# A hybrid convolution decoder step on one core: a reciprocal in three pieces and another order of low parts, weight sums and swishes

## What is computed

```python
proj = jnp.einsum('btd,de->bte', z, w_in)
a_val, a_glu, a_gate, b_h, b_c, b_b, b_gate, m_a, m_b = jnp.split(proj, SPLIT_IDX, axis=-1)
u_a = a_val * jax.nn.sigmoid(a_glu)
c_a, new_buf_a = causal_dwconv(buf_a, u_a, conv_a_w)          # width 31
c_a = layernorm(c_a + conv_a_b, ln_a_g, ln_a_b)
y_a = jax.nn.silu(c_a) * jax.nn.silu(a_gate)
u_b = b_c * b_h
c_b, new_buf_b = causal_dwconv(buf_b, u_b, conv_b_w)          # width 3
y_b = b_b * c_b * jax.nn.silu(b_gate)
merged = (jax.nn.sigmoid(m_a) * jnp.einsum('btc,cd->btd', y_a, w_pa)
          + jax.nn.sigmoid(m_b) * jnp.einsum('btc,cd->btd', y_b, w_pb))
h = h + jnp.einsum('btd,de->bte', merged, w_out)
```

## Time and profile before

| | |
|---|---|
| median of 3 runs | 1069.04 us (1068.72 to 1070.01) |
| the profiled execution | 1069.02 us |
| its span in the profile | 1067.2 us |
| instructions in the span | 19847 |
| granted clock of PE over the span, share of full speed | 0.992 |
| chain that ended last, share of the span | PE 85%, DVE 5%, DMA 3%, ACT 3%, issue 2% |
| DMA | 181.03 MB, mean 170 GB/s |

### The profile page before, as it was taken

One profiled execution on the slowest core, in us unless ns is written; L12 is line 12 of the kernel. 1 busy time (PEld: TensorE's weight loads), 2 busy tenths in 40 slices (PEclk: granted clock), 3 DMA queues, 4 the chain that ended last, 5 costly groups with the idle time before them and its releaser, 6 DMA issues.

```text
span 1067.2 us, 19847 instructions
## 1 busy us (share of the span) xinstructions
PE 1025.9 (96%) x7948; PEld 998.0 (94%) x7948; DVE 829.4 (78%) x904; ACT 471.8 (44%) x725; POOL 519.0 (49%) x369
## 2 busy tenths in 40 slices
PE   5899999999999999999999999799998988999997
PEld 5899999999999999999999999799998988998885
DVE  6779989899998989899996674875595489765523
ACT  7654343434434343433444555556463354242311
POOL 3166566565655656566563553445564456420000
PEclk9999999999999999999999999899998999999999
DMA  8677666657656665665656464584946646455321
GB/s 266 173 163 182 153 170 156 170 128 192 154 149 175 157 168 130 186 157 147 173 149 204 140 211 138 180 272 156 316 149 216 211 120 208 154 195 177 119 81 41
DMA packets 183535, 181.03 MB, mean 170 GB/s; under 512 B 9135, under 2 KB 145455, under 8 KB 182404
## 3 DMA queue, kind: packets, MB, share of 16 engines
q1 hardware_dynamic: 168468, 152.50, 44.5%
q0 software_dynamic: 14976, 27.27, 14.2%
HBM read 118.46 MB, written 35.00 MB: 144 GB/s over the span
## 4 chain that ended last, share of the span: by engine, by line
PE 85%; DVE 5%; DMA 3%; ACT 3%; issue 2%; POOL 1%; SPq 1%; ACTq 0%; DVEq 0%
PE pp L2020 74%; PE pp L2180 8%; DMA sgb<-m_spill 2%; DVE big L1506 1%; DVE xop L1469 1%; PE pp L2037 1%; POOL wop L918 1%; PE spare L2196 1%; DVE big L1948 1%; ACT wop L1017 1%; DVE ring L1664 1%; DVE x_stage L1458 1%; DMA x_stage<-in_x_prompt_dram 1%; ACT wop L985 0%; ACT xop L1001 0%
## 5 line engine op out<-in xcount | busy, mean ns | idle before, releaser
L2020 PE MATMUL pp<-xop,wop 128*128 128x262 f32 (+1 forms) x7224 | 892.1, 285 | 22.1 <-issue 7.5
L2020 PEld LDWEIGHTS pp<-xop,wop 128*128 128x128 f32 x7224 | 885.3, 190 | 26.8 <-issue 15.8
L918 POOL TENSOR_TENSOR wop<-ring,wop 128x512 fp32r<-128x512 f32 (+1 forms) x256 | 442.4, 1733 | 389.3 <-ACT wop L985 384.8
L985 ACT ACTIVATE wop<-ring 128x512 fp32r<-128x512 f32 (+1 forms) x262 | 181.6, 698 | 233.0 <-PE pp L2020 232.9
L1575 DVE SCALAR_TENSOR_TENSOR big<-big,cst 128x513 f32<-128x513 f32 x112 | 107.8, 963 | 0.7
L2180 PE MATMUL pp<-xop,wop 128*128 128x512 f32 x384 | 89.2, 394 | 0.0
L2180 PEld LDWEIGHTS pp<-xop,wop 128*128 128x128 f32 x384 | 72.0, 188 | 16.8
L1586 DVE SCALAR_TENSOR_TENSOR spare<-big,tap_sum,spare 128x512 f32<-128x512 f32 x112 | 83.7, 748 | 0.3
L1575 DVE SCALAR_TENSOR_TENSOR spare<-big,cst,spare 128x512 f32<-128x512 f32 x112 | 83.6, 746 | 0.0
L1677 DVE TENSOR_TENSOR big<-big,pp 128x524 f32<-128x524 f32 (+1 forms) x43 | 29.8, 693 | 45.9 <-PE pp L2020 45.1
L1664 DVE TENSOR_TENSOR ring<-ring 128x512 f32<-128x512 f32 x68 | 64.3, 985 | 0.0
(11 more groups left out here) (127 smaller groups left out, 713.5 us busy)
## 6 DMA issues: line engine op xcount, KB each, us to landing
ring<-in_w_in_dram SPq DMA_DIRECT2D x222, 256.0 KB, 3.3
ring<-ring POOLq DMA_DIRECT2D x104, 256.0 KB, 4.4
big<-c_spill SPq DMA_DIRECT2D x16, 516.0 KB, 5.1
big<-yb_spill SPq DMA_DIRECT2D x5, 1032.0 KB, 9.5
big<-ya_spill SPq DMA_DIRECT2D x5, 1032.0 KB, 8.0
m_spill<-big SPq DMA_DIRECT2D x16, 262.0 KB, 4.4
yb_spill<-big SPq DMA_DIRECT2D x8, 516.0 KB, 5.4
c_spill<-big SPq DMA_DIRECT2D x8, 516.0 KB, 4.5
```

The costliest lines, as they stand in the source:

```text
L918: G.tensor_tensor(wop[:, s0:s1, 1, :], raw, f(wop[:, s0:s1, 0, :]), ALU.subtract).then_inc(wlo, 1)
L985: A.activation(wop[:, s0:s1, 0, :], raw, ACT.Copy).then_inc(whi, 1)
L2020: last = T.matmul(out, wop[:, s, wp, P * k:P * (k + 1)], xop[s][:, xp, k, n * ch:n * (ch + 1)], start=(s in FRESH and k == 0 and m == 0), ...
```

## The change

It changes the order of instructions on ACT and DVE in units 29, 30, 35, 36, 39 and 40, and splits one instruction in three.

- The reciprocal at the end of unit 29 is made in three pieces of 344 columns, each of which waits for its own third of the square roots. The multiply of the first normalize_c waits for all three.
- In unit 30 norm_swish(0) and norm_swish(1) move on ACT: the first from ahead of the wait for slot 1 to behind act_first (ahead of the fourth snapshot), the second from ahead of the third snapshot to behind w_hi(31, 3).
- In units 35 and 39 x_high(p, 0) moves on ACT ahead of the first snapshot. On DVE x_low(p, 0) moves ahead of c11, and x_sum(p, 2) from ahead of c22 to behind it.
- In units 36 and 40 weight_sum 0 for the next unit moves behind x_low(p, 4), weight sums 1 to 3 from behind c11 to behind c22 (and the multiply that follows it), x_low(p, 5) ahead of the multiply that follows c11, and x_low(p, 6) ahead of the multiply and the sums that follow c22.

```diff
--- before.py
+++ after.py
@@ -1303,6 +1303,10 @@
                 more = v < NU
                 if kind == "short":
                     conv_begin(i)
+                if u == NZ - 1:
+                    x_high(1, 0)
+                if u == NPB - 1:
+                    x_high(2, 0)
                 first_product(u)
                 if u == 1:
                     x_high(0, 4)
@@ -1319,20 +1323,14 @@
                     square_row(4)
                 if n == 4:
                     square_row(7)
-                if n == 5:
-                    norm_swish(0)
                 if n == 6:
                     norm_swish(3)
                 if n == 7:
                     norm_swish(5)
                 if n == 8:
                     norm_swish(7)
-                if u == NZ - 1:
-                    x_high(1, 0)
                 if u == NZ:
                     x_high(1, 5)
-                if u == NPB - 1:
-                    x_high(2, 0)
                 if u == NPB:
                     x_high(2, 5)
 
@@ -1354,8 +1352,6 @@
                     mean_row(1)
                 if n == 3:
                     square_row(5)
-                if n == 5:
-                    norm_swish(1)
                 if u == NZ - 1:
                     x_high(1, 1)
                 if u == NPB - 1:
@@ -1371,6 +1367,8 @@
                     stage_sigmoids(i, 1)
                 if n == 1:
                     mean_row(2)
+                if n == 5:
+                    norm_swish(0)
                 if n == 2:
                     square_row(2)
                 if n == 3:
@@ -1392,6 +1390,7 @@
                 if more:
                     w_hi(v, 3)
                 if n == 5:
+                    norm_swish(1)
                     norm_swish(2)
                 if n == 6:
                     norm_swish(4)
@@ -1831,7 +1830,7 @@
                     w_low(5)
                 if u > 1:
                     after_c21(u - 1)
-                if VSUM <= u + 1 < NU:
+                if VSUM <= u + 1 < NU and u not in (NZ, NPB):
                     weight_sum(u + 1, 0)
                 if kind == "gate":
                     conv_b(i)
@@ -1848,23 +1847,27 @@
                     normalize_c(1)
                 if u == NZ - 1:
                     x_sum(1, 1)
+                    x_low(1, 0)
                 if u == NPB - 1:
                     x_sum(2, 1)
+                    x_low(2, 0)
                 if u == NZ:
                     x_low(1, 4)
+                    weight_sum(u + 1, 0)
                 if u == NPB:
                     x_low(2, 4)
+                    weight_sum(u + 1, 0)
 
 
                 c11(u)
                 if u == 1:
                     x_low(0, 5)
-                after_c11(u)
                 if u == NZ:
                     x_low(1, 5)
                 if u == NPB:
                     x_low(2, 5)
-                if VSUM <= u + 1 < NU:
+                after_c11(u)
+                if VSUM <= u + 1 < NU and u not in (NZ, NPB):
                     for step in (1, 2, 3):
                         weight_sum(u + 1, step)
                 if kind == "gate":
@@ -1892,13 +1895,9 @@
                 if n == 8:
                     gate_c(6)
                 if u == NZ - 1:
-                    x_low(1, 0)
                     x_low(1, 1)
-                    x_sum(1, 2)
                 if u == NPB - 1:
-                    x_low(2, 0)
                     x_low(2, 1)
-                    x_sum(2, 2)
 
                 if u == LAST:
                     wo_low(0)
@@ -1911,7 +1910,14 @@
                 c22(u)
                 if u == LAST:
                     wo_low(3)
+                if u == NZ:
+                    x_low(1, 6)
+                if u == NPB:
+                    x_low(2, 6)
                 after_c22(u)
+                if u in (NZ, NPB):
+                    for step in (1, 2, 3):
+                        weight_sum(u + 1, step)
                 if kind == "short":
                     sample_a(i)
                 if spread:
@@ -1919,13 +1925,11 @@
                 if n == 8:
                     gate_c(7)
                 if u == NZ - 1:
+                    x_sum(1, 2)
                     x_sum(1, 3)
                 if u == NPB - 1:
+                    x_sum(2, 2)
                     x_sum(2, 3)
-                if u == NZ:
-                    x_low(1, 6)
-                if u == NPB:
-                    x_low(2, 6)
 
 
                 c12(u)
@@ -1944,9 +1948,11 @@
                     add_square(5)
                     center(7)
                 if n == 4:
-                    dve.wait_ge(std_ready, 3)
-                    V.reciprocal(rstd, rstd).then_inc(rstd_ready, 1)
-                    dve.wait_ge(rstd_ready, 1)
+                    n3 = TOK // 3
+                    for ch in range(3):
+                        dve.wait_ge(std_ready, ch + 1)
+                        V.reciprocal(rstd[:, n3 * ch:n3 * (ch + 1)], rstd[:, n3 * ch:n3 * (ch + 1)]).then_inc(rstd_ready, 1)
+                    dve.wait_ge(rstd_ready, 3)
                     normalize_c(0)
                 if n == 5:
                     gate_c(1)
```

## The result

The changed kernel takes 1078.16 us (median of 4 runs, 1076.94 to 1079.07), the kernel before beside it 1069.53 (1068.72 to 1071.81): 1.0064 times as long, 95% interval 1.0048 to 1.0080, some 6.9 us; the two medians by themselves are 8.6 apart. Predicted were 1075.1, in 1066.0 to 1079.5, and slower as the likeliest case. The profiled execution took 1079.07, 10.05 more than that of before, with a span of 1077.2 and a mean granted clock of 0.985.

What follows compares the result with a forecast made beforehand. PE was busy 96% of the span, so only its idle time could be won, stage by stage. Terms -0.6 + 2.9 + 3.8 = +6.1 on 1069.04 gave 1075.1 us, range 1066.0 to 1079.5.

Steps and rivals of the forecast that it cites:

- Units 29 and 30, -0.6: Product 4 of unit 30 on time, product 6 idle 4.3 behind c22, clock halved; -0.6 us in all.
- POOL's turns: Unit 30: DVE and POOL alternate at the port; POOL's weight parts add 1.2 to the subtract, 2.3 to the multiply.
- A split: Unit 30: DVE and POOL share port bandwidth instead of turns; unit 30 ends near 678.5, the whole at 1070.4 us.
- Rival (a): Unit 30: normalize_c(2)'s subtract reaches the port before POOL, -5.1 instead of -0.6; 1070.6 us, chance 0.18.
- its bound of -5.1: Units 29 and 30: with the subtract ahead of POOL, idle before product 6 is 1.9, the clock holds, -5.1 us.
- Units 35 to 38, +2.9: Late weight sums hold SP's sigmoid loads; PE idles 5.2 before product 2 of unit 37, clock falls; +2.9 us.
- Rival (b): Staged-sigmoid loads of units 36 to 38 land in 2.6: +2.9 becomes -0.8, +3.8 becomes -0.5; 1067.1 us, chance 0.14.
- Units 39 to 41, +3.8: x_high(2,0) delays 39/2, late sums delay load_old(0) and merges: +2.8 with clock held, +1.0 for the clock; +3.8 us.
- the clock at 39/2: Product 2 of unit 39: after 3.8 of idle a clock fall costs 2.0; half taken, +1.0 us.
- The bounds between which I put that chance: Unit 39: idle of 3.8 lies between 2.1, which held the clock, and 4.33, which did not.
- the load: Unit 40: load_old(0) goes at 902.0 instead of 897.31, lands 907.4, delaying the merges and 41/3; +2.8 with clock held.
- Rival (c): Nothing queues behind the late sums and all places gain: -5.1, -3.5 and -2.4; 1058 us, chance 0.10.

Runs made afterwards that it cites:

- p1_c22_first: Kernel before with only the part of units 29 and 30, plus normalize_c(2) moved behind c22 on DVE in unit 30: 1065.48 us, ratio 0.9943.
- a_whi3_late: Changed kernel with ACT's w_hi(31, 3) moved behind norm_swish(2), making POOL's weight parts late: 1075.46 us, ratio 1.0026 to the kernel before.
- p3_only: Kernel before with only the change's part of units 36 and 40 (low parts ahead of weight sums): 1077.95 us, ratio 1.0070.
- a_sgb_first: Changed kernel with SP's store and staged-sigmoid loads of unit 36 ahead of the rb21 and rb22 loads: 1077.23 us, ratio 1.0062 to the kernel before.
- best4: Changed kernel with best3's SP and quadrant order, c22 ahead of normalize_c(2), load_old(0) ahead of rb21, x_high(2,0) behind unit 39's first snapshot: 1062.69 us, ratio 0.9921.
- a_xhigh_back: Changed kernel with x_high(2,0) in unit 39 back behind the first snapshot on ACT: 1075.99 us, ratio 1.0041 to the kernel before.
- p1_only: Kernel before with only the change's part of units 29 and 30 (reciprocal in thirds, two swishes moved): 1070.15 us, ratio 0.9992.
- p2_only: Kernel before with only the change's part of units 35 and 39 (x_high, low part 0 and x_sum moved): 1075.65 us, ratio 1.0048.
- a_old_first: Changed kernel with SP's load_old(0) in unit 40 ahead of the load of rb21: 1077.35 us, ratio 1.0049 to the kernel before.
- best3: p1_c22_quads with SP's stores and sigmoid loads put ahead of the rb21 and rb22 loads in units 36 to 39: 1061.14 us, ratio 0.9905 to the kernel before.
- order_only: best3 with the pass 2 quadrant loads back in their places of the kernel before: 1058.05 us, ratio 0.9877 to the kernel before.
- p1_c22_quads: p1_c22_first with the four quadrant loads of pass 2 put off on SP to the ends of units 37 and 38: 1068.79 us, ratio 0.9976 to the kernel before.

## Why the prediction was right, term by term

**Units 29 and 30, -0.6: measured -0.77.** 30/4 was due on time and came on time, 30/6 after an idle of 4.3 and came after 3.75; the clock fell. Adding 1.2 and 2.3 for POOL's turns gave 2.4 and 3.5 for the two instructions, measured 2.33 and 3.26. A split, with unit 31 near 678.5, fell: it started at 683.97. Rival (a), DVE first at the port, fell; p1_c22_first and a_whi3_late show that the collision is what kept 5 us from being won, as its bound of -5.1 had it. Their shares differ: 7.0 won in unit 30 with c22 ahead, 5.0 with POOL made late.

**Units 35 to 38, +2.9: measured +3.83** (38/2 against 31/0, where the two traces are 0.16 apart). The chain came row by row as written: sums to 810.24 (predicted 810.1), L601 at 811.59 (811.15), staged at 815.54 (815.65), L601 at 816.00 (816.0), staged at 821.61 (821.05), idle 5.41 (5.2), 37/3 4.3 later than before (3.8). p3_only shows that the late sums of units 36 and 40 alone cost 1.0070, a_sgb_first that unit 37's stall hangs on the queue, best4 that the sums cost nothing that can be told once the queue is another. The mis-sized rest is 0.5 at 37/2 and 37/3, and 0.4 at 38/2, which the prediction had on time: the first snapshot stood behind sigmoid loads again, the first of them landing 11.0 after its issue behind the quadrants. Rival (b), quick landings, fell: the two took 3.3 and 5.0.

**Units 39 to 41, +3.8: measured +5.14** (41/3 against 38/2). Without the clock the term was 2.8, made of 39/2 (+1.9 predicted, +1.91 measured), 40/2 (+0.5 more, measured +0.78), 40/6 (-2.8, measured -2.74) and 41/3 (+3.2, measured +2.86): within 0.4 each. The mis-sized step is the clock at 39/2. I had put half of 2.0 on it; with an idle of 3.67 (predicted 3.8) it fell whole, and 39/3 came 5.30 after 39/2 instead of 2.97: +2.33 in place of +1.0. In a_xhigh_back the idle is 0.71 and the clock held, so the stall is the cause; x_high(2,0) makes 1.91 of it and the landing of the load the rest. The bounds between which I put that chance do not hold either. The idle that "held it" is 1.91, 2.1 being the length of the window, and other traces lost the clock after 1.91 (p1_only) and 1.98 (p2_only) and held it after 2.35 (41/3 of the changed kernel) and 2.57 (36/6 of p2_only). In p1_only, where units 35 to 41 are as before, it fell at 39/2 after 2.85 and at 40/6 after 1.91, and 38/2 to 41/3 took 73.27 where the trace of before has 70.70. So up to half of the 5.14 can be luck of the trace of before; the medians and the experiments carry the result, not this term. For 41/3 the prediction named the load, which was right in the changed kernel; a_old_first shows that the port stands right behind it.

**What the sum did not have.** +0.96 in units 41 and 42: load_old(1) (L646 at 922.56) went 13.2 behind 41/0 (10.0 before) and landed 9.1 after its issue (7.6 before), the merges of unit 41 began at 931.71, and 42/1 was 0.8 late; the prediction followed only load_old(0). And +0.93 ahead of unit 30 in this one execution: 30/0 started at 655.76, at 655.18 with the same first part in p1_only, at 654.90 in best3 and at 654.83 before, so it is scatter of the start-up. The terms give -0.77 + 3.83 + 5.14 + 0.96 = 9.16 for the two traces; the medians differ by 8.6, and the ratio of 1.0064 is 6.9, near the 6.1 of the prediction.

One more reading of the prediction is off and changes no term: the clock fell not 2.5 but 2.3 into the idle ahead of 36/6, since that idle began at 804.83 and not with the window at 804.60.

Rival (c), nothing queues, fell in all three places. Another order of SP came to 1058 as well (order_only); that the numbers agree is chance, since order_only leaves out the moves in units 35 to 40 that the rival counted on.

## What to carry to other kernels

When work is moved later on an engine, list who waits for it on every queue that is served in order, and what stands behind that waiting DMA: here three sums, moved out of the way of the low parts, held a load that 37/2 needed, and the new stall (5.41) was longer than what the move took from the old one (4.33 to 0.97). Put DMAs that gate the next few microseconds ahead of those that wait or that move a megabyte; that order alone took the ratio from 0.9943 to 0.9877 here. Where two engines slow each other, as DVE and POOL do here, move the instruction that others wait for out of the collision and leave the collision itself.

## What the runs showed of the hardware

- The collision of DVE and POOL keeps its price: a multiply of 1032 columns took 1.23 alone and 3.26 to 3.33 beside POOL's 1024-column weight part, in all eleven kernels that have the reciprocal in three. Moving POOL's parts only handed it on to the next multiply (a_whi3_late).
- The length of an idle does not tell by itself whether the clock falls. Ahead of 40/6 PE was idle 1.91 before, and the clock stayed at 2.4 GHz; in p2_only it was idle 1.98 at the same place, and the 24 matmuls behind took 4.48 at a mean clock of 0.62. In p1_only, where that place is as before, the idle was 1.91 too, and 41/0 came 4.29 after 40/6. In the changed kernel an idle of 2.35 ahead of 41/3 left the next product at 2.98. So 1.3 to 1.5 us at this place differ from one kernel's profile to another without an edit there.
- A load of sgb (128x516) landed 2.7 to 3.4 us after its issue in half of order_only's twelve cases, and 9 to 11 behind two loads of a quadrant (page, part 6, big<-ya_spill: 1032.0 KB, median 7.5) in the changed kernel, p1_c22_quads, best3 and best4.
